# A router's end in a new order: low parts first, the last tile in halves, slot tokens ahead of two weight splits

## The reference, cut to what matters

```python
x = layer_norm(ALPHA * x + mix, ln1_g[i], ln1_b[i])
g_logits = xt @ w_group + b_group              # 4 groups: the best one
e_logits = xt @ w_expert + b_expert            # 16 experts: the two best of that group
hgu = einsum("td,edf->tef", xt, w_gate_up); gate, up = split(hgu, 2)
y = einsum("tef,efd->td", silu(gate) * up * combine, w_down)
x = layer_norm(ALPHA * x + y, ln2_g[i], ln2_b[i])
x = x + sigmoid(x @ ple_w_gate[i] + ple_b_gate[i]) * (p[i] @ ple_w_proj[i])
# mixer B: y = (gate_b * conv3(gate_c * hx)) @ w_out
```

## Time and profile before

| | |
|---|---|
| runs | 1280.24, 1276.55, 1279.85 us, median 1279.85 |
| profiled execution | 1276.34 us, of which 1274.70 is the span of the trace |
| granted TensorE clock, mean | 0.991 of 2.4 GHz |
| busy share | PE 97%, DVE 65%, ACT 44%, POOL 13% |
| chain that ended last | PE 68%, DVE 14%, DMA 11%, ACT 3%, issue 2%, POOL 1% |

### The profile page before, as it was taken

How to read it: one execution, slowest core, us unless ns; L and a number is a source line. 1 busy time by engine, 2 the same in 40 slices (tenths; PEclk the granted TensorE clock), 3 DMA queues, 4 the chain that set the end, 5 groups by cost and what they waited for, 6 DMA issues and landing times.

```text
span 1274.7 us, 19729 instructions
## 1 busy us (share of the span) xinstructions
PE 1231.9 (97%) x7707; PEld 1118.5 (88%) x7707; DVE 834.9 (65%) x1118; ACT 558.6 (44%) x627; POOL 165.1 (13%) x193
## 2 busy tenths in 40 slices
PE   7999999999999999999999999999999899999998
PEld 6888899999999998788778799999998788877698
DVE  4554477464574746789889785445434879889793
ACT  4322232213131223378888564112121368888651
POOL 2200010010000002013331001000002012232100
PEclk9999999999999999799999999999999989999999
DMA  9444354243241322369998553322322359999612
GB/s 340 152 158 156 103 156 148 88 157 115 83 152 59 138 79 102 146 257 377 374 380 322 197 168 103 100 67 84 115 69 85 141 193 366 387 396 347 224 51 75
DMA packets 85616, 229.76 MB, mean 180 GB/s; under 512 B 9798, under 2 KB 42702, under 8 KB 73136
## 3 DMA queue, kind: packets, MB, share of 16 engines
q1 hardware_dynamic: 66880, 179.84, 39.1%
q0 software_dynamic: 18672, 49.04, 10.7%
HBM read 210.15 MB, written 35.46 MB: 193 GB/s over the span
## 4 chain that ended last, share of the span: by engine, by line
PE 68%; DVE 14%; DMA 11%; ACT 3%; issue 2%; POOL 1%; DVEq 0%; SPq 0%; ACTq 0%; POOLq 0%
PE ps L1739 14%; PE ps L1741 14%; PE ps L1740 14%; DMA w_raw<-in_moe_w_gate_up 9%; DVE w_lo L1169 4%; PE ps L1790 3%; PE ps L1792 3%; PE ps L1791 3%; ACT w_hi L853 2%; PE ps L2077 2%; PE ps L2079 2%; PE ps L2078 2%; PE ps L1850 2%; DVE x_tok L1568 1%; DMA ln_params<-in_ln_b 1%
## 5 line engine op out<-in xcount | busy, mean ns | idle before, releaser
L1169 DVE TENSOR_TENSOR w_lo<-w_raw,w_hi 128x2048 fp32r<-128x2048 f32 (+1 forms) x133 | 290.6, 2191 | 69.6 <-ACT w_hi L853 69.1
L1739 PE MATMUL ps<-x_hi,w_hi 128*128 128x288 f32 (+2 forms) x1024 | 304.8, 298 | 5.2 <-DVE w_lo L1169 3.7
L1741 PE MATMUL ps<-x_hi,w_lo 128*128 128x288 f32 (+2 forms) x1024 | 302.3, 295 | 0.0
L1740 PE MATMUL ps<-x_lo,w_hi 128*128 128x288 f32 (+2 forms) x1024 | 302.2, 295 | 0.0
L853 ACT ACTIVATE w_hi<-w_raw 128x2048 fp32r<-128x2048 f32 (+1 forms) x133 | 242.8, 1834 | 79.5 <-PE ps L1741 61.8
L1739 PEld LDWEIGHTS ps<-x_hi,w_hi 128*128 128x128 f32 x1024 | 193.2, 189 | 7.0 <-DVE w_lo L1169 4.4
L1740 PEld LDWEIGHTS ps<-x_lo,w_hi 128*128 128x128 f32 x1024 | 193.2, 189 | 0.1
L1741 PEld LDWEIGHTS ps<-x_hi,w_lo 128*128 128x128 f32 x1024 | 193.1, 189 | 0.0
L1739 PE MATMUL ps<-g_hi,w_hi 128*128 128x288 f32 x384 | 114.9, 299 | 3.4 <-DVE g_full L1715 2.7
L1741 PE MATMUL ps<-g_hi,w_lo 128*128 128x288 f32 x384 | 113.9, 297 | 0.0
L1740 PE MATMUL ps<-g_lo,w_hi 128*128 128x288 f32 x384 | 113.8, 296 | 0.0
(11 more groups left out here) (297 smaller groups left out, 2138.4 us busy)
## 6 DMA issues: line engine op xcount, KB each, us to landing
w_raw<-in_moe_w_gate_up SPq DMA_DIRECT2D x34, 1024.0 KB, 10.8
w_raw<-in_moe_w_down SPq DMA_DIRECT2D x32, 1024.0 KB, 13.8
w_raw_more<-in_moe_w_gate_up SPq DMA_DIRECT2D x30, 1024.0 KB, 14.5
w_raw<-in_a_w_in SPq DMA_DIRECT2D x23, 1024.0 KB, 5.3
w_raw<-in_a_w_out SPq DMA_DIRECT2D x12, 1024.0 KB, 5.0
w_raw<-in_b_w_in SPq DMA_DIRECT2D x12, 1024.0 KB, 5.1
w_raw<-in_ple_w_gate SPq DMA_DIRECT2D x8, 1024.0 KB, 12.0
v_scratch<-v_stage POOLq DMA_DIRECT2D x6, 1024.0 KB, 4.6
```

Of the source, the lines that this page charges most:

```text
L1169: dve.tensor_tensor(unit_of(wlo, d), raw_unit(d), unit_of(whi, d).bitcast(f32), ALU.subtract).then_inc(split_done, 1)
L1739: pe.matmul(out, sh, mh, start=first, stop=False)
L1740: pe.matmul(out, sh, ml, start=False, stop=False)
L1741: ins = pe.matmul(out, sl, mh, start=False, stop=final)
```

## The change: what it does

- Mixer B: the split that stood behind the third product (fl = 2) stands behind the fourth.
- PE: `h_turns(3)` goes between the two halves of tile 4's products, the first group's logit turns behind the first half. Tile 4 is turned in two halves of four transposes (`last_turns`), and its logits come in two halves (`last_logits`). The ranks of group 0 go behind the turns. Projection tiles are spread: order 1, 0, 3, 2, 4 to 7 (`PROJ_ORDER`), and half tiles cut in parts (k0, k1).
- ACT: tile 4's high part in two halves behind the first projection copy.
- DVE: `select` is cut in `places_of` and `marks_of`; tile 3's low part goes ahead of tile 4's statistics; the last step of tile 4's norm and its low part go in halves; `lo(U_E + 1)` and `lo(U_E + 2)` go behind the slot tokens and the overflow's tables.

```diff
@@ ACT
+                def last_rows_hi():
+                    act.wait_ge(r_mm, NT * l + NT - 2)
+                    for h, (turned_ok, done) in enumerate(((ht_half, hh_half), (ht_ok, hh_ok))):
+                        act.wait_ge(turned_ok, (l + 1) if h == 0 else NT * (l + 1))
+                        act.activation(hTh[0][:, 4 * h:4 * h + 4, 0:TS], turned_half(h), ACT.Copy).then_inc(done, 1)
...
-                rows_hi(4)
+                proj_out(1)
+                last_rows_hi()
                 logits_copy(1)
-                proj_out(1)
                 proj_out(0)
                 hi(U_E[l] + 1)
+                proj_out(3)
                 proj_out(2)
                 hi(U_E[l] + 2)
-                for mo in range(3, KT - 1):
+                for mo in range(4, KT - 1):
@@ DVE
+                def norm_last():
...
+                    for h, done in enumerate((nz_half, nz_ok)):
+                        c = slice(512 * h, 512 * h + 512)
+                        dve.scalar_tensor_tensor(out=xtok[0:TS, i, c], in0=xtok[0:TS, i, c], scalar=rstd[0:TS, i:i + 1], in1=lnp[0:TS, 1, c],
+                                                 op0=ALU.mult, op1=ALU.add).then_inc(done, 1)
+                def last_rows_lo():
+                    for h, (hi_ok, done) in enumerate(((hh_half, hl_half), (hh_ok, hl_ok))):
...
-                select(*GROUPS[0])
+                places_of(*GROUPS[0])
+                rows_lo(3)
                 stats_of(4)
-                norm_of(4)
-                rows_lo(3)
-                rows_lo(4)
+                norm_last()
+                marks_of(*GROUPS[0])
+                last_rows_lo()
                 slots_of(*GROUPS[0])
-                select(*GROUPS[1])
+                places_of(*GROUPS[1])
+                marks_of(*GROUPS[1])
                 slots_of(*GROUPS[1])
-                lo(U_E[l] + 1)
                 dve.wait_ge(ab_used, l + 1)
...
-                lo(U_E[l] + 2)
...
+                lo(U_E[l] + 1)
+                lo(U_E[l] + 2)
@@ DVE, mixer B
-                            if fl < 3:
-                                lo(U_B + 4 * r + fl + AHEAD)
+                            if fl != 2:
+                                lo(U_B + 4 * r + min(fl, 2) + AHEAD)
@@ PE
                 h_turns(2)
+                row_products(4, 0, range(ROUND))
                 logit_turns(0)
-                row_products(4, 0, range(ROUND))
+                h_turns(3)
                 row_products(4, 1, range(ROUND)).then_inc(mt_done, KT - NT + 1)
-                h_turns(3)
                 pe.wait_ge(pl_ok, 3 * l + 3)
                 logits(2)
-                ranks(0)
-                pe.wait_ge(nz_ok, 2 * NT * l + NT - 1)
                 proj_half(l, 1, 0)
                 proj_half(l, 1, 1).then_inc(mt_done, 1)
-                h_turns(4)
                 logits(3)
-                logits(4)
-                pe.wait_ge(nz_ok, 2 * NT * l + NT)
+                last_turns()
+                ranks(0)
                 proj_half(l, 0, 0)
+                last_logits()
+                proj_half(l, 0, 1, 0, 1)
                 logit_turns(1)
-                proj_half(l, 0, 1).then_inc(mt_done, 1)
+                proj_half(l, 0, 1, 1, 2).then_inc(mt_done, 1)
+                pe.wait_ge(pp_done, KT * l + 1)
+                proj_half(l, 3, 0)
+                proj_half(l, 3, 1).then_inc(mt_done, 1)
+                pe.wait_ge(pp_done, KT * l + 2)
+                proj_half(l, 2, 0)
                 ranks(1)
                 slot_products(0)
-                pe.wait_ge(pp_done, KT * l + 2)
-                proj_half(l, 2, 0)
+                proj_half(l, 2, 1).then_inc(mt_done, 1)
                 slot_products(1).then_inc(ab_used, 1)
-                proj_half(l, 2, 1).then_inc(mt_done, 1)
-                for mo in range(3, KT - 1):
+                for mo in range(4, KT - 1):
                     proj(l, mo)
```

More of the change, by code:

```diff
@@ L348, in trunk @@
         ht_ok, hh_ok, hl_ok = sem("x1_turned"), sem("x1T_hi_ready"), sem("x1T_lo_ready")
+        nz_half, ht_half = sem("x1_half_normed"), sem("x1_half_turned")
+        hh_half, hl_half = sem("x1T_hi_half_ready"), sem("x1T_lo_half_ready")
         lt_cp, lt_ok = sem("logits_copied"), sem("logits_turned_back")
@@ L426, in turned, with turned_half @@
             return ps[:, 4:6, :].rearrange("p b (k t) -> p (b k) t", t=P)[:, :, 0:tok(i)]
+        def turned_half(h):
+            return ps[:, 4 + h, :].rearrange("p (k t) -> p k t", t=P)[:, :, 0:TS]
         def p_parts(dst, g):
@@ L497, in wait_used @@
                 eng.wait_ge(vps_done, it * (NT * step // 2) + NT * (d // 2 - 1))
+        PROJ_ORDER = (1, 0, 3, 2, 4, 5, 6, 7)
         TR_IN = 0
@@ L1336, in norm_of @@
                                              op0=ALU.mult, op1=ALU.add).then_inc(nz_ok, 1)
+                def norm_last():
+                    i, b = NT - 1, rows_bank(NT - 1)
+                    dve.wait_ge(st_ok, NT * (l + 1))
+                    dve.scalar_tensor_tensor(out=xtok[0:TS, i, :], in0=ps[0:TS, b:b + 2, :].rearrange("p b t -> p (b t)"), scalar=mv[0:TS, i, 0:1],
+                                             in1=lnp[0:TS, 0, :], op0=ALU.subtract, op1=ALU.mult).then_inc(rs_ok, 1)
+                    dve.wait_ge(sq_ok, 1 + n1 + NT)
+                    ch.link(dve.reciprocal(rstd[0:TS, i:i + 1], rstd[0:TS, i:i + 1]))
+                    dve.wait_ge(rs_ok, 1 + n1 + NT)
+                    for h, done in enumerate((nz_half, nz_ok)):
+                        c = slice(512 * h, 512 * h + 512)
+                        dve.scalar_tensor_tensor(out=xtok[0:TS, i, c], in0=xtok[0:TS, i, c], scalar=rstd[0:TS, i:i + 1], in1=lnp[0:TS, 1, c],
+                                                 op0=ALU.mult, op1=ALU.add).then_inc(done, 1)
                 def p_low(g):
@@ L1345, in rows_lo, with places_of @@
                     dve.tensor_tensor(hTl[i % 2][:, :, 0:tok(i)], turned(i), hTh[i % 2][:, :, 0:tok(i)].bitcast(f32), ALU.subtract).then_inc(hl_ok, 1)
+                def last_rows_lo():
+                    for h, (hi_ok, done) in enumerate(((hh_half, hl_half), (hh_ok, hl_ok))):
+                        dve.wait_ge(hi_ok, (l + 1) if h == 0 else NT * (l + 1))
+                        dve.tensor_tensor(hTl[0][:, 4 * h:4 * h + 4, 0:TS], turned_half(h), hTh[0][:, 4 * h:4 * h + 4, 0:TS].bitcast(f32),
+                                          ALU.subtract).then_inc(done, 1)
                 lg20 = lg[:, :, :, :].rearrange("p t g j -> p t (g j)")
-                def select(a, b):
+                def places_of(a, b):
                     n, g = b - a, (0 if a == 0 else 1)
@@ L1367, in select, with marks_of @@
                                               in_=won.rearrange("p q c i -> p q (c i)"), op=ALU.add, axis=AX.X))
+                def marks_of(a, b):
+                    n = b - a
                     place = rank_c[:, 5 * a:5 * b, :].rearrange("p (t g) j -> p t g j", g=5)
@@ L1946, in logits, with last_turns, last_logits @@
                     ins.then_inc(r_mm, 1)
+                def last_turns():
+                    pe.wait_ge(hl_ok, NT * l + NT - 1)
+                    for h, (normed, done) in enumerate(((nz_half, ht_half), (nz_ok, ht_ok))):
+                        pe.wait_ge(normed, (l + 1) if h == 0 else 2 * NT * l + NT)
+                        for k in range(4 * h, 4 * h + 4):
+                            ins = pe.transpose(ps[:, 4 + h, (k % 4) * P:(k % 4) * P + TS], xtok[0:TS, NT - 1, k * P:k * P + P], ident[0:TS, 0:TS])
+                        ins.then_inc(done, 1)
+                def last_logits():
+                    out = ps[0:RW, 7, P * (NT - 1 - GROUPS[1][0]):P * (NT - 1 - GROUPS[1][0]) + TS]
+                    for h, lo_ok in enumerate((hl_half, hl_ok)):
+                        pe.wait_ge(lo_ok, (l + 1) if h == 0 else NT * (l + 1))
+                        for k in range(4 * h, 4 * h + 4):
+                            pe.matmul(out, wrp[:, k, :], hTh[0][:, k, 0:TS], start=(k == 0), stop=False)
+                            ins = pe.matmul(out, wrp[:, k, :], hTl[0][:, k, 0:TS], start=False, stop=(k == KT - 1))
+                    ins.then_inc(r_mm, 1)
                 def logit_turns(g):
@@ L2043, in turn_slots, with proj_half @@
                         ins.then_inc(xtp, 1)
-            def proj_half(l, mo, h):
+            def proj_half(l, mo, h, k0=0, k1=2):
                 if h == 0:
@@ L2048, in proj_half @@
                 return products(ps[:, 2 * (mo % 2) + h, 0:HALF], [(wp(whi, mo // 2, k, P * (mo % 2)), wp(wlo, mo // 2, k, P * (mo % 2)),
-                                                                 gview(pThi, k, h), gview(pTlo, k, h)) for k in range(2)])
+                                                                 gview(pThi, k, h), gview(pTlo, k, h)) for k in range(k0, k1)],
+                                k0 == 0, k1 == 2)
             def proj(l, mo):
@@ L2053, in proj @@
                     pe.wait_ge(split_done, U_P[l] + mo // 2 + 1)
```

(3 more changed lines are left out.)

2 lines of the change are left out of this document (1 added, 1 removed).

## The result

The changed kernel takes 1262.88 us (median of 4 runs, 1262.63 to 1264.46); the kernel before, timed beside it, 1279.18 (1276.55 to 1280.24). The ratio is 0.9878, with a 95% interval of 0.986 to 0.9896: 16.3 us less. The profiled execution of the changed kernel took 1262.75, its span is 1261.2.

A forecast was written before the change was run, and what follows sets the result against it. It took the urgent line from tile 4 to the first expert as the bound. Gains of 5.9 (layer 0), 4.9 (layer 1) and 3.7 (mixer), 14.5 from 1276.34, gave 1261.8, with noise 1263.5; range 1259 to 1267.

The forecast's parts named there:

- The half of 3.5 us: Added to the sum: the profiled execution lay 3.5 under the median; half went to noise, raising 1261.8 to 1263.5.
- Step 1: Layer 0's router: tile 4's statistics start at 519.2, not 518.34, since eight transposes now stand inside tile 4's products.
- Steps 2 to 5: Layer 0's router, tile 4's norm through logits, selection and ranks to VectorE's read of slot products: 533.6, before 538.28.
- just in time: Layer 0, ahead of the ranks: 21 projection matmuls, 2.9 us, done at 529.95, with ranks at 530.05.
- Step 6: Slot products to first expert, three lines: VectorE's 542.7 taken as last, PE 541.3, gather 541.8 to 543.4.
- The gather, the least certain term: Before the first expert: lands 4.0 to 5.6 after its instruction starts, 4.0 if alone; at 5.6 expert 0.7 later a layer.
- brings little: Router: moving the first weight split alone gains little, as it held VectorE's read some 0.5 us; uncovered, both splits cost 4.4.
- The mixer: Layer 1's mixer: wait of 2.67 for the fourth product goes, 0.8 for an addition comes; gain 3.7, about 1.8 clock.
- Clock at half in part of the way: Rival, chance 0.2: new gaps at the gather and before the expert drop the clock in part of the routers; 1268.
- The experts' stage: Rival, chance 0.1: this stage, bound by its weight stream, gives the gain back; 1268.4.
- the bound of 1 us: Sign of a wrong prediction: the experts' stage longer than before by over 1 us.
- The slower case: Rival, chance 0.03: clock at half from tile 4's logits to the first expert in both layers; 1279.0.

The follow-up runs named there:

- e1: The kernel before, with only mixer B's split moved behind the fourth product: 1274.94 us, ratio 0.9968.
- e4: The kernel before, with only the two expert weight splits moved behind the slot tokens and the overflow's tables: 1277.45 us, ratio 0.9992.
- e5: The changed kernel with its projection tiles in their old order, twelve matmuls fewer ahead of the second ranks: 1270.59 us, ratio 0.9946.
- e10: The changed kernel with only the first of the two expert weight splits put back, ahead of VectorE's read of the slot products: 1270.52 us, ratio 0.9944.
- e3: The changed kernel with both expert weight splits put back to their old places on VectorE: 1276.15 us, ratio 0.9979.
- e12: The changed kernel with the mixer's moved split put later still, ahead of the third addition in the round that adds: 1264.40 us, ratio 0.9892.
- e11: The kernel before, with idle matmuls filling TensorE's router gaps and both expert weight splits moved behind the tokens: 1273.62 us, ratio 0.9962.
- e9: The changed kernel with both expert weight splits put back, and SP's released weight loads held until the first gather has landed: 1268.95 us, ratio 0.9934.
- e6: The kernel before, with idle matmuls that nobody reads filling TensorE's gaps in the router: 1275.26 us, ratio 0.9979.

## Why the prediction was right, and where it wasn't

**The forecast** was 1263.5; the median is 1262.88. From profile to profile it had 14.5 less, and 13.6 came (1276.34 to 1262.75). The half of 3.5 us that it gave for the low profiled time of before wasn't needed: the new order lacks most of the half clock that differs from run to run, and its median is 0.13 above its profiled time. So the 1.7 added for noise covered the 0.9 by which the sum was too low, and that the total came within 0.6 is in part luck; the steps are the better test.

**Step 1** is off by half a microsecond: statistics at 519.76, not 519.2. They wait 0.36 for TensorE's last products, so the transposes in front of these, and not VectorE, set them. But the half microsecond isn't theirs: the profiled run is already 0.47 later at tile 2's low part (514.54, before 514.07), ahead of all that the change moves, and the same code reaches tile 4's statistics at 518.34 in the kernel before, 518.46 in e1 and 519.83 in e4. Layer 0's 5.4 in place of 5.9 is this difference from run to run. **Steps 2 to 5** hold within 0.15 each, counted from the statistics: norm halves to 4.35 (4.2), logits 6.8 (6.8), selection 7.9 (8.0), ranks 10.8 (10.85), slot products 13.5 (13.55), read 14.4 (14.4). The steps came so close because each was a count of instructions at a duration of the row before. That the spread keeps the ranks "just in time" was right, and e5 puts its price at 7.7, of which the prediction had given none.

**Step 6**: VectorE's line ends last, as taken: TensorE's first expert matmul waits 0.45 for the low part. The gather, the least certain term, took 4.4 to the turned slots, between the ends of 4.0 and 5.6 and near the low one. The prediction's reason, that it is now alone on the DMA engines, is borne out by e10, where a load ahead of it costs 0.7 and 1.3. The rule of the Trainium skill that it weighed there (DMA: Bandwidth & Descriptors, Issuing engines are not separate DMA queues) agrees with this.

**The part that failed** is the sentence that the move of the first split alone "brings little", 0.5 us, with 4.4 for both splits in the new place if the gather didn't cover them. For the kernel before it is true (e4: nothing). For the changed kernel the term was mis-sized and two mechanisms were missing: moved back, the splits cost 13 us, because VectorE reads 1.15 us later, the second split then holds the gather's instruction on GpSimd for 1.2 us, the load that the first releases goes ahead of the gather, and the clock falls in the long wait. The forecast didn't suffer, since the new order avoids both.

**The mixer**: 3.7 was predicted with 0.8 for a new wait on an addition. The wait is 0.68, the product isn't waited for, the stretch up to layer 1's statistics lost 3.34 with the later statistics (0.86) in it, by the prediction's count, so about 4.2; e1 by itself gave 3.6.

**The rivals.** Clock at half in part of the way didn't occur in the changed kernel's routers; it is a part of e5's 7.7 and of e3's 13. Its ground was read too simply: the prediction gave layer 0's fall to the gap of 1.85 ahead of tile 4's turn, but layer 1 of the same trace has a longer gap at the same place, which it doesn't name, and the clock stayed at 2.4 GHz behind it:

```profile
1010.54 0.68 PE L1935 MATMUL ps<-ident,x_tok 64*128 64x64 f32 x8 [2.02 <-DVE x1T_lo L1345]
```

The experts' stage gave back nothing in layer 0 (first to last turned activation 146.9 before, 146.8 after) and 1.0 in layer 1 (146.6 and 147.7), just at the bound of 1 us that the prediction had set; this is most of the difference between 14.5 and 13.6. It doesn't look like an effect of the order: the same stretch of layer 1 takes 146.1 in e12, whose router is the changed one, and 147.4 and 147.9 in e4 and e11, whose router has the old order on TensorE. What makes it differ from run to run stays open. The slower case needed half clock through both routers, which no kernel with the new order showed.

## What to carry to other kernels

The worth of moving a piece of work is that of the line which ends last at that moment: the same two splits were worth 0 in one order and 13 us in the other, so price an edit again after each edit that shortens another line. Look at what a piece of work does beside its own engine: a split on VectorE held an instruction on GpSimd and released a load, and both hit the transfer that everything waited for. And fill of low urgency (here the projection) is best cut into the gaps of the urgent line, where it keeps the clock up, rather than put behind it.

## What the runs showed of the hardware

- GpSimd's indirect DMA instruction took 1.12 us alone and 2.33 to 2.37 where a 2.28 us VectorE split had begun before it, ending 0.98 to 0.99 after the split in e3 and e9. In e6 the second gather's instruction took 2.64 and 2.69 in the same position, ending 0.89 after the split. Where it had begun before the split, it took 1.00 to 1.12.
- The gather's slots were turned 4.4 us after its instruction began with nothing beside it, 5.2 to 5.6 with one 1 MB load issued 1.1 us ahead, 7.5 to 8.0 with that load, a held instruction and a second load.
- The clock's fall doesn't follow from the length of the gap alone. It stayed up through 3.05 in e9's layer 0, 2.83 in e10's and 2.02 in layer 1 of the kernel before, fell about the end of 3.26 and 3.20 in layer 1 of e9 and e10, and fell after 1.85 in layer 0 of the kernel before. Even the same gap in front of the same matmul, near the end of layer 1, goes both ways. TensorE's timeline in the changed kernel, where the clock stayed at 2.4 GHz, and in e12, where it went to 1.2 for some 3.4 us from about 1216:

```profile
1216.46 0.39 PE L1776 MATMUL ps<-x_hi,w_hi 128*128 128x256 f32 x1 [1.83 <-DVE w_lo L1182]
```

```profile
1214.48 0.39 PE L1778 MATMUL ps<-x_hi,w_hi 128*128 128x256 f32 x1 [1.82 <-DVE w_lo L1182]
```

So kernels that differ by under 2 us here are told apart by the place that changed, not by one run's total.
